# Paged keys of a decode step turned on VectorE in 32 by 32 blocks instead of on TensorE

## The chip, the cores and the metric

One core of one Trainium2 chip. The metric is the device time of one execution in microseconds, the median of several runs. All arithmetic is fp32, so each matmul stands in the trace as two MATMUL and two weight-load instructions (a transposition as one of each).

## The reference

Two layers of a hybrid decoder run over a prompt of 256 rows and over 8 sequences ("samples") that each add one token to 1024 cached ones. The cache is paged: 8 pages of 128 rows for each sequence. For the samples a layer computes two attentions over the cached keys, one attention over a band of the last 512 keys, and a compression of cached keys and values in blocks of 32 rows:

```python
full = jnp.concatenate([past_rows, rows], axis=1)
fdk, fdv, fik, fck, fcv, fsk, fsv = _split(full, CACHE_SPLITS)
yb = _dsa_attend(dq_h, iq_h, iw, qpos, fdk, fdv, fik)          # scores q . fdk
ck = _compress(fck, cmp_pe[0], cmp_w1[0], cmp_b1[0], cmp_w2[0])
cv = _compress(fcv, cmp_pe[1], cmp_w1[1], cmp_b1[1], cmp_w2[1])
o_cs = _nsa_cmp_sel(nq_h, qpos, ck, cv, fsk, fsv)              # scores q . fsk
o_w = _window_attend(nq_h, qpos, wk, wv, pos0 + L - lw)        # scores q . wk, 512 keys

def _compress(kv, pe, w1, b1, w2):
    blk = kv[:, idx] + pe[:, None, :]        # 63 blocks of 32 rows, step 16
    return jax.nn.silu(blk @ w1 + b1) @ w2
```

Keys have two heads of 64 columns, so a page has 128 columns of each of fdk, fsk, fck and fcv; there are 8 query heads for each sequence.

## The kernel before

Each engine has its own program, written out by hand, and they meet at semaphores (named steps such as "T 7", "C 7", "h 2"). A layer runs: the norm (ScalarE squares L1378, TensorE sum over partitions L782, ScalarE logarithm and exponential L1380 and L1382, VectorE scaling L1748), projections of slabs of w_in (L814), prompt work with gate projections (`mix`, L967) between its pieces, the page stage, the samples' softmax and output, the branches (L1322) and the output projection (L1340). Slabs of weights rotate through three slots; SP sends the slab for a slot once the last user of the slab three places before in the list STREAM is done.

**The page stage** is a loop over NW = 40 windows, 5 for each sequence. Four of them take a pair of pages each, the fifth takes the band of 512 keys.

- SP loads the even pages and POOL the odd ones into four slots `kst` (L549, L550: 64 KB and 192 KB each). A slot is loaded again as soon as TensorE has turned what it held ("T w").
- TensorE, in a page window: 8 transpositions of 128x128 (L1220), 4 of attention keys (into bank 3 or 5) and 4 of compression rows (into bank 4 or 6); then the scores of the window before, against its turned keys `KT` (L1175, L1179: 2 matmuls with 128 rows, 64 queries and 256 columns, one for each half of the output partitions). In a band window: 4 transpositions (L1224).
- ScalarE copies the turned keys from PSUM to `KT` (128x512, L1365), and half of the compression rows (two copies of 64x256, L1365) into `cT`; VectorE copies the other half (two of 64x256, L2125). TensorE may turn window w only when the copies of window w-2 are done.
- Compression goes by pairs of sequences: once a pair is in `cT`, TensorE multiplies it by `w1` in the page windows of the next sequence (`compress`, L1190: 4 matmuls of 256 columns in each of 4 windows). ScalarE moves one half of the result (`shift`), VectorE adds it (`join`, L2116), ScalarE applies SiLU (`hidden`, L1625), TensorE multiplies by `w2` (`compressed`, L1198, L1202), ScalarE takes the result. The last pair's `compress` has nothing beside it (L1190, 16 matmuls), and its end, "h 3", releases the loads of the values of sequences 4 to 7 (L556, L567), because they overlap `cT`.
- VectorE does some comparing for the sparse attention's choice of keys between its copies (L1931 to L1961).

ScalarE's first copy into `cT` of a layer waits until the second of two spills of gate projections (POOL, L741) has landed.

Of the kernel before, what the change touches and what calls it, by code (L numbers as in the profile page):

```python
# [14 lines left out]
ALU = mybir.AluOpType  # L15
# [3 lines left out]
D = 1024  # L19
LP = 256  # L20
NS = 8
# [7 lines left out]
NH = 8  # L29
# [13 lines left out]
NU = 5  # L43
NW = NS * NU
# [60 lines left out]
STREAM = ([n for n in FRONT + BACK + GATES if n in SLAB_OF] + [s[0] for s in GATE_SLABS] + [s[0] for s in OUT_SLABS])  # L105
NSLOT = 3


def slab_dmas(name):

    if name in SLAB_OF:
# [100 lines left out]
def hybrid_step(nc, x_prompt, x_sample, cache_kv, page_table, state_win, state_hgrn, norm_g, w_in,  # L212
# [4 lines left out]
    with ctx:  # L217
# [108 lines left out]
        cT = at(8192, 2, 2, ST, 4 * NBLK)  # L326
        Vw = at(16384, NS, 4, 128)
        kst = at(18432, 4, 2, 512)
        kws = at(22528, 2, 4, 128)
        KT = at(23552, 2, 512)  # L330
        hbd = at(24576, 8, NCS)[0:HD]
        hsd = at(25080, 8, NCS)[0:HD]
        hid = at(25584, 2, 2, 2, NCS)[0:HD]
# [21 lines left out]
        spill = nc.dram_tensor("spill", [2, 128, KD * LT], F32, kind="Internal").ap()  # L355
        xr = at(24000, 2, D)
# [17 lines left out]
        class Steps:  # L374
# [15 lines left out]
            def mark(self, step):  # L390
# [15 lines left out]
        first_in, lb_in = sem("first_in"), sem("lb_in")  # L406
        nx_p = Steps("nx_p", [f"xT {k}" for k in range(KD)])
# [42 lines left out]
        pg_p = Steps("pg_p", sum([[f"T {w}"] + [f"s {w - 1}"] * (w > 0) for w in range(NW)], []) + [f"s {NW - 1}"])  # L450
        pg_a = Steps("pg_a", sum([[f"K {w}"] + [f"C {w}"] * (w % NU < 4) for w in range(NW)], []))
        pg_v = Steps("pg_v", [f"C {w}" for w in range(NW) if w % NU < 4])
        GR = list(range(NS // 2))
        dc_p = Steps("dc_p", sum([[f"h {g}", f"w {g}"] for g in GR[:-1]], [])
                     + ["h 3", "new", "w 3", "s cmp", "t cmp", "imp", "group imp", "PT", "oT"])
        dc_v = Steps("dc_v", [f"sum {g}" for g in GR] + ["s cmp", "n cmp", "ptx cmp", "imp", "drop", "masked", "new p", "scaled", "ev"])
        dc_a = Steps("dc_a", sum([[f"hb {g}", f"hid {g}", f"c {g}"] for g in GR[:-1]], []) + ["scores", "hb 3", "hid 3", "c 3"]
# [53 lines left out]

        def blocks_of(s, k, u):

            return cT[halves[u], s // 2 % 2, :, :, :].rearrange("p v t (g b n) -> p v g b n t", g=2, b=2)[:, :, :, s % 2, 16 * k:16 * k + 16, :]
# [43 lines left out]
        def first_keys(engine, l, odd, pages):  # L558
# [3 lines left out]
            load_values(engine, l, 0, odd, pages)  # L562

# [6 lines left out]
        def _(sp):  # L570
# [21 lines left out]
            for l in range(DEPTH):  # L592
                l1 = bass.ds(l, 1)

                def send(name):
# [5 lines left out]
                    if at_ >= NSLOT:  # L601

                        old = STREAM[at_ - NSLOT]
                        if old in SLAB_OF:
                            sp.wait_ge(proj_ready, l * NJOB + LAST_JOB[old])
                        elif old[0] == "m":
# [50 lines left out]
                for name in ("m13", "m20", "m21", "m22"):  # L657
                    send(name)
                sp.wait_ge(cp_v.sem, cp_v(l, "prompt done"))
                for s in range(NS):  # L660
# [5 lines left out]
                    if s >= 2:  # L666
                        sp.wait_ge(pg_p.sem, pg_p(l, f"T {(s - 2) * NU + 4}"))
                    sp.dma_start(kws[:, s % 2, :, :], sw[:, :, 0:128]).then_inc(win_in[s % 2], 16)
                    if s in (2, 4, 6):
                        load_values(sp, l, s // 2, 0, pages)  # L670

                sp.wait_ge(dc_p.sem, dc_p(l, "h 3"))
                for s in range(4, NS):
                    load_values(sp, l, s, 0, pages)
                for name in ("m23", "b00", "b01"):
                    send(name)
# [19 lines left out]
        def _(pool):  # L696
# [8 lines left out]
            for l in range(DEPTH):  # L705
# [31 lines left out]
                for a in range(2):  # L737
                    pool.wait_ge(mx_a.sem, mx_a(l, f"m {8 * a + 7}"))
# [9 lines left out]
                for s in range(NS):  # L748
# [4 lines left out]
                    if s in (2, 4, 6):  # L753
# [1537 lines left out]
```

## Time and profile before

| | us |
|---|---|
| median of 3 runs | 1210.1 |
| lowest and highest | 1209.66, 1226.07 |
| the profiled execution, device time | 1212.78 |
| its span, first to last instruction | 1210.8 |
| TensorE matmul busy | 1115.8 (92%) |
| VectorE busy | 557.1 (46%) |
| ScalarE busy | 442.6 (37%) |
| chain that ended last, share on TensorE | 74% |

Busy time of TensorE counts a matmul from start to end, and matmuls overlap, so 92% doesn't say that the array is full. What an engine costs at a place is read from the chain of waits: the time from one group of instructions to the next. The two layers have the same program; the second one's page stage lies 594 us after the first one's.

### The profile page before, as it was taken

How to read it: one execution, taken by the hardware profiler on the slowest of the kernel's cores; microseconds unless marked ns; L12 is line 12 of the kernel's file. 1: busy time of each engine (PE TensorE's matmuls, PEld its weight loads, DVE VectorE, ACT ScalarE, POOL GpSimd, SP SyncE). 2: the span in 40 equal slices, each digit the busy share in tenths (PEclk: the TensorE clock that was granted, in tenths of full speed). 3: DMA queues.
4: the chain of work that ended last, by engine and by line, in shares of the span. 5: the costliest groups of instructions: out<-in, count | busy, mean ns of one | idle time of the engine just before them, and what ended most of it. 6: DMA issues, size and time to landing. Idle time of an engine off the chain costs nothing.

```text
span 1210.8 us, 19137 instructions
## 1 busy us (share of the span) xinstructions
PE 1115.8 (92%) x6856; PEld 884.6 (73%) x6856; DVE 557.1 (46%) x1306; ACT 442.6 (37%) x882; POOL 188.7 (16%) x327
## 2 busy tenths in 40 slices
PE   6999998998898899899789999899989979989998
PEld 4887777876675667788578877698657656668887
DVE  2103277878565542314111134887876563432241
ACT  2123442246433775320011353322654256652100
POOL 0200040011111451400020001200202044422000
PEclk8999998999998999999899999999999999999999
DMA  6563257545465784855345633683636287837552
GB/s 174 156 138 109 86 177 245 138 115 158 124 187 169 237 239 127 244 166 150 87 106 157 144 117 88 232 206 105 179 94 199 90 255 226 252 102 210 164 146 71
DMA packets 242716, 192.79 MB, mean 159 GB/s; under 512 B 117822, under 2 KB 224350, under 8 KB 241342
## 3 DMA queue, kind: packets, MB, share of 16 engines
q1 hardware_dynamic: 227358, 140.38, 42.4%
q0 software_dynamic: 15264, 51.19, 13.0%
q8 instruction: 55, 0.90, 0.3%
q14 instruction: 39, 0.32, 0.1%
HBM read 179.10 MB, written 20.80 MB: 165 GB/s over the span
## 4 chain that ended last, share of the span: by engine, by line
PE 74%; ACT 8%; DVE 7%; issue 3%; DMA 2%; DVEq 2%; SPq 2%; ACTq 1%
PE ps L814 21%; PE ps L967 11%; PE ps L1322 7%; PE ps L1190 5%; PE ps L1340 5%; ACT arena L1365 4%; PE ps L1220 4%; PE ps L990 2%; PE ps L1175 2%; PE ps L1101 1%; DMA spill<-arena 1%; PE ps L1293 1%; SPq L526 1%; PE ps L857 1%; DVE top L1807 1%
## 5 line engine op out<-in xcount | busy, mean ns | idle before, releaser
L1365 ACT ACTIVATE arena<-ps 64x256 f32<-64x256 f32 (+9 forms) x374 | 204.9, 564 | 285.3 <-PE ps L1332 73.7
L814 PE MATMUL ps<-hT,slab 128*128 128x264 f32 (+1 forms) x1280 | 300.5, 393 | 9.0 <-DVE hT L1748 6.4
L814 PEld LDWEIGHTS ps<-hT,slab 128*128 128x128 f32 (+1 forms) x1280 | 244.7, 193 | 54.4 <-issue 9.4
L967 PE MATMUL ps<-hT,slab 128*128 128x264 f32 x768 | 184.3, 397 | 3.3 <-DVEq L2100 3.3
L967 PEld LDWEIGHTS ps<-hT,slab 128*128 128x128 f32 x768 | 146.5, 194 | 36.0 <-issue 6.8
L2125 DVE COPY arena<-ps 64x256 f32<-64x256 f32 x128 | 76.1, 594 | 88.8 <-PE ps L1220 87.4
L539 POOL DMA_DIRECT2D arena<-in_cache_kv_dram x64 | 34.5, 539 | 397.2 <-PE ps L911 240.8
L1322 PE MATMUL ps<-Y,slab 128*128 128x264 f32 x384 | 85.8, 386 | 0.0
L1220 PE MATMUL ps<-cst,arena 128*128 128x128 f32 x512 | 70.7, 284 | 16.2 <-ACT arena L1365 9.3
L1220 PEld LDWEIGHTS ps<-cst,arena 128*128 128x128 f32 x512 | 58.4, 144 | 34.3 <-ACT arena L1365 21.1
L1322 PEld LDWEIGHTS ps<-Y,slab 128*128 128x128 f32 x384 | 73.0, 190 | 12.5
L1759 DVE SCALAR_TENSOR_TENSOR arena<-arena,gains 128x264 f32<-128x264 f32 x26 | 11.0, 488 | 117.2 <-ACT arena L1437 117.2
L1340 PE MATMUL ps<-arena,slab 128*128 128x264 f32 x256 | 62.2, 400 | 2.3 <-DVEq L2243 2.3
L1190 PE MATMUL ps<-arena,w 128*128 128x256 f32 x256 | 62.9, 393 | 0.0
L1513 ACT ACTIVATE arena<-ps 128x264 f32<-128x264 f32 x48 | 18.7, 389 | 113.1 <-PE ps L967 112.5
L1340 PEld LDWEIGHTS ps<-arena,slab 128*128 128x128 f32 x256 | 50.1, 198 | 11.8 <-DVEq L2243 3.1
L1190 PEld LDWEIGHTS ps<-arena,w 128*128 128x128 f32 x256 | 47.0, 192 | 15.9 <-issue 10.4
L556 POOL DMA_DIRECT2D arena<-in_cache_kv_dram x64 | 45.2, 711 | 43.0 <-PE ps L1190 41.0
L549 POOL DMA_DIRECT2D arena<-in_cache_kv_dram x64 | 34.4, 538 | 109.2 <-PE ps L1175 56.7
L1560 ACT ACTIVATE arena<-arena,st 128x128 f32<-128x128 f32 (+1 forms) x96 | 42.4, 444 | 13.7 <-DVEq L2023 12.9
L1175 PE MATMUL ps<-arena,QC 128*64 128x256 f32 x256 | 42.7, 413 | 2.3 <-ACT arena L1365 2.3
L1365 ACT ACTIVATE Y<-ps 128x264 f32<-128x264 f32 x24 | 9.4, 390 | 93.5 <-PE ps L814 93.5
(380 smaller groups left out, 1385.7 us busy)
## 6 DMA issues: line engine op xcount, KB each, us to landing
slab<-in_w_in_dram SPq DMA_DIRECT2D x48, 1024.0 KB, 5.5
slab<-in_w_in_dram SPq DMA_DIRECT2D x80, 256.0 KB, 3.9
arena<-in_cache_kv_dram SPq DMA_DIRECT2D x64, 192.0 KB, 3.8
arena<-in_cache_kv_dram POOLq DMA_DIRECT2D x64, 192.0 KB, 3.9
arena<-in_cache_kv_dram SPq DMA_DIRECT2D x64, 128.0 KB, 5.1
arena<-in_cache_kv_dram POOLq DMA_DIRECT2D x64, 128.0 KB, 5.7
slab<-in_w_branch_dram SPq DMA_DIRECT2D x16, 512.0 KB, 5.6
slab<-in_w_out_dram SPq DMA_DIRECT2D x8, 1024.0 KB, 4.8
```

What stands on the lines that cost most here:

```text
L539: engine.dma_start(ikst[:, u, i, h * HD:h * HD + HD], page_rows(l, pages[2 * pair + h, i])[:, 256:320])\
L556: engine.dma_start(V[:, s, 2 * k + odd, :, :], key_and_selected(pg, 128)).then_inc(v_in[odd], 16)
L814: last = mm(ps[0:job[3], n % 2, 0:LT], v[:, k, job[2]:job[2] + job[3]], hT[:, k, :], start=(k == 0), stop=(k == KD - 1))
L967: last = mm(ps[:, bank, 0:LT], v[:, k, (d % 2) * 128:(d % 2) * 128 + 128], hT[:, k, :], start=(k == 0), stop=(k == KD - 1))
L1175: last = mm(ps[h, j // 2, (j % 2) * 256:(j % 2) * 256 + 256], QC[:, a, s * ROWS:(s + 1) * ROWS], KT[:, w % 2, a * 256:(a + 1) * 256], star ...
L1190: last = mm(ps[:, 7, kv * 256:(kv + 1) * 256], w1[:, kv, t, :], cT[:, g % 2, kv, t, :], start=(t == 0), stop=(t == ST - 1))
L1220: last = nc.tensor.transpose(ps[:, bank, o:o + 128], kst[:, u % 4, i, c:c + 128], ident)
L1322: last = mm(ps[:, d % 4, 0:LT], v[:, j, dd * 128:dd * 128 + 128], Y[:, a, j, :], start=(j == 0), stop=(j == 3))
L1340: last = mm(ps[:, d % 4, 0:LT], v[:, k, (d % 2) * 128:(d % 2) * 128 + 128], mT[:, k, :], start=(k == 0), stop=(k == KD - 1))
L1365: return A(out, in_, ACT.Copy, scale=scale)
L1560: A(x[:, j, :], x[:, j, :], ACT.Exp, bias=st[:, c + j:c + j + 1], accum_out=sa[:, c + j:c + j + 1])
L2125: last = TC(blocks_of(s, j, u)[:, :, 0], pairs_of(4 + 2 * (w % 2), 0, u))
```

## The change

**Keys.** The attention keys of pages are no longer turned by TensorE. VectorE turns `kst` in blocks of 32 by 32, within each group of 32 partitions, into `kD` (two transpositions of 128x256 for a page window, step "D u"), and the band of a sequence in one transposition of 128x512 (step "W s"). After that, partition 32r+x holds column 32c+x of the tokens of row group r. Scores of a sequence are made at once, in `page_scores(s)`: for each of 4 column chunks c, each of 4 row groups r and each of 2 attentions a, one matmul with 32 rows, 32 queries and 256 (a=0) or 384 columns (a=1: pages and band), into bank r at the quarter 2a + s//4. It is called in the second window of the next sequence and waits for "W s". Its queries lie in `QR`, which POOL builds (a memset of 2048 columns, 16 copies) in a weight slot: the name "qr" is put into STREAM ahead of "m21", so later slabs move by one slot, "m22" is sent after the page stage, and "m23" waits for the last scores.

**Windows.** 32 windows, 4 for each sequence; 4 transpositions in each (compression rows only, banks 4 and 5). A `kst` slot is loaded again after both "T u" and "D u". ScalarE has no copy to `KT`.

**Compression** goes by sequence: 4 matmuls of 128 columns in every window of the next sequence, two banks (6 and 7) by turns, `compressed` for each sequence but the last two inside the loop. `cT` is halved.

**Values.** Those of sequence 1 are loaded during the prompt's work (`second_values`), of 2 and 3 at sequences 3 and 5.

**Elsewhere.** TensorE does 9 matmuls on a tile of zeros at the start and 7 at the start of each layer, before it waits for the first scaled hT (`keep_busy`). ScalarE does one dummy logarithm at the start of each layer.

```diff
+            pe.wait_ge(idle_set, 1)
+            keep_busy(5, 9)
...
+                                    if k == 0:
+                                        keep_busy(5, 7)
                                     pe.wait_ge(norm_v.sem, norm_v(l, f"hT {k}"))
...
+                def page_scores(s):
+
+                    pe.wait_ge(pg_v.sem, pg_v(l, f"W {s}"))
+                    for c in range(4):
+                        for r in range(4):
+                            for a in range(2):
+                                out = ps[quarter[2 * a + s // 4], r, 0:(NPG + 4 * a) * 32].rearrange("p (n j) -> p n j", j=32)
+                                last = mm(out, queries_of(r, c, a, s), block_keys(s, a)[quarter[r], :, 32 * c:32 * c + 32],
+                                          start=s % 4 == 0 and c == 0, stop=s % 4 == 3 and c == 3)
+                    last.then_inc(pg_p.sem, pg_p.mark(f"s {s}"))
...
+                for u in range(NU):
+                    s, j = u // 4, u % 4
+                    for e in range(2):
+                        pe.wait_ge(page_in[j][e], (l * NS + s + 1) * 32)
+                    if u >= 2:
+                        taken_from(u - 2)
+                    for a, c in enumerate((128, 256)):
+                        for i in range(2):
+                            o = a * 256 + i * 128
+                            last = nc.tensor.transpose(ps[:, 4 + u % 2, o:o + 128], kst[:, j, i, c:c + 128], ident)
+                    last.then_inc(pg_p.sem, pg_p.mark(f"T {u}"))
+                    if s:
+                        if j == 2 and s >= 2:
+                            compressed(s - 2)
+                        compress(s - 1, j)
+                        if j == 1:
+                            page_scores(s - 1)
+                for part in range(2):
+                    compress(NS - 1, part)
+                page_scores(NS - 1)
+                for part in range(2, 4):
+                    compress(NS - 1, part)
+                compressed(NS - 2)
...
                 if s:
-                    engine.wait_ge(pg_p.sem, pg_p(l, f"T {(s - 1) * NU + k}"))
+                    engine.wait_ge(pg_p.sem, pg_p(l, f"T {u - 4}"))
+                    engine.wait_ge(pg_v.sem, pg_v(l, f"D {u - 4}"))
...
+                A(spare[:, :], epsb[:, :], ACT.Ln)
...
+                ve.wait_ge(spill_out[0], l * 16 + 16)
+                for w in range(NU):
+                    s, j = w // 4, w % 4
+                    if s >= 2 and j == 0:
+                        ve.wait_ge(dc_p.sem, dc_p(l, f"h {s - 2}"))
+                    ve.wait_ge(pg_p.sem, pg_p(l, f"T {w}"))
+                    for u in range(2):
+                        last = TC(blocks_of(s, j, u)[:, :, 0], pairs_of(4 + w % 2, 0, u))
+                    last.then_inc(pg_v.sem, pg_v.mark(f"C {w}"))
+                    if s >= 2 and j == 0:
+                        ve.wait_ge(pg_p.sem, pg_p(l, f"s {s - 2}"))
+                    for a, c in enumerate((0, 384)):
+                        last = nc.vector.transpose(block_keys(s, a)[:, 2 * j:2 * j + 2, :], kst[:, j, :, c:c + 128])
+                    last.then_inc(pg_v.sem, pg_v.mark(f"D {w}"))
+                    if j == 3:
+                        ve.wait_ge(win_in[s % 2], (l * 4 + s // 2 + 1) * 16)
+                        nc.vector.transpose(block_keys(s, 1)[:, NPG:NPG + 4, :], kws[s % 2]).then_inc(pg_v.sem, pg_v.mark(f"W {s}"))
+                        if s:
+                            join(s - 1)
```

## Rows read from the trace of the kernel before

**Rows 1.** Page, first parts: busy us, share of the span, instructions

```profile
PE 1115.8 (92%) x6856; PEld 884.6 (73%) x6856; DVE 557.1 (46%) x1306; ACT 442.6 (37%) x882; POOL 188.7 (16%) x327
```

**Rows 2.** Stretches: us from start, length, busy (count) by engine, granted clock, DMA share, GB/s

```profile
379.00:485.00 106.00, 95.65 (x626) 67.56 (x628) 45.50 (x87) 72.00 (x125) 40.84 (x71) 0.98 0.70 211
```

**Rows 3.** The chain that ended last, page stage: start us, us, what

```profile
375.59 8.35 DMA spill<-arena
...
403.74 1.92 PE ps L1190 x8
405.67 0.87 PE ps L1220 x8
406.54 0.58 PE ps L1175 x4
...
428.84 1.93 PE ps L1190 x8
...
445.14 0.64 PE ps L1198 x4
445.78 0.60 PE ps L1202 x8
...
477.46 7.10 PE ps L1190 x32
```

**Rows 4.** Instruction groups of 379 to 485 us: busy us, mean ns | idle before

```profile
L1365 ACT ACTIVATE arena<-ps 64x256 f32<-64x256 f32 x66 | 39.7, 602 | 3.6 <-DMA spill<-arena 2.5
L2125 DVE COPY arena<-ps 64x256 f32<-64x256 f32 x64 | 38.0, 594 | 43.7 <-PE ps L1220 43.0
L1365 ACT ACTIVATE arena<-ps 128x512 f32<-128x512 f32 x40 | 23.8, 594 | 21.6 <-PE ps L1220 21.2
```

**Rows 5.** The chain elsewhere: full matmuls, four column groups

```profile
199.45 1.78 PE ps L990 x16
...
516.24 3.61 PE ps L1293 x128
```

**Rows 6.** Timeline of TensorE: a matmul in each of four row groups

```profile
370.38 0.73 PE L1158 MATMUL ps<-arena 24*128 24x264 f32 x8
```

**Rows 7.** Timeline of VectorE, instructions of 256 to 513 elements

```profile
390.84 0.41 DVE L1931 TENSOR_SCALAR tk<-tk,sgn,tkv 104x257 f32<-104x257 f32 x1
391.17 0.41 DVE L1932 TENSOR_SCALAR tk<-tk,sgn,tkv 104x257 f32<-104x257 f32 x1
...
398.77 0.69 DVE L1957 TENSOR_TENSOR_SCAN tk<-cst,tk 104x257 f32<-104x257 f32 x1
...
488.52 0.67 DVE L2157 TENSOR_REDUCE st<-arena 64x1 f32<-64x513 f32 x1
```

**Rows 8.** Page, DMA issues: KB each, us from issue to landing

```profile
arena<-in_cache_kv_dram POOLq DMA_DIRECT2D x64, 192.0 KB, 3.9
```

**Rows 9.** Timeline of POOL: a key load issued; a memset at the start

```profile
1.58 1.05 POOL L700 MEMSET QC<- 128x1152 f32 x1
...
404.45 0.55 POOL L549 DMA_DIRECT2D arena<-in_cache_kv_dram  x1
```

**Rows 10.** Start of each layer: first matmul (timeline), chain, one stretch

```profile
8.00 0.66 PE L790 MATMUL ps<-cst,arena 128*128 128x128 f32 x2 [8.00 <-DMA arena<-in_x_sample_dram]
...
15.51 6.18 PE ps L782 x16
...
24.64 21.08 PE ps L814 x80
...
25.00:30.00 5.00, 5.00 (x12) 3.77 (x12) 3.07 (x11) 0.21 (x1) 0.00 (x0) 0.50 0.10 15
...
619.25 1.28 ACT L1380
...
623.47 19.73 PE ps L814 x80
644.98 24.92 PE ps L814 x112
```

More of the change, by code:

```diff
@@ L42 @@
 ROWS = NS * NH
-NU = 5
-NW = NS * NU
+NU = NS * 4
 ST = CS // 2
@@ L355, in hybrid_step @@
         spill = nc.dram_tensor("spill", [2, 128, KD * LT], F32, kind="Internal").ap()
+        idle = at(30400, LT)
         xr = at(24000, 2, D)
@@ L656, in _ @@
                 first_keys(sp, l, 0, pages)
-                for name in ("m13", "m20", "m21", "m22"):
+                for name in ("m13", "m20"):
                     send(name)
+                second_values(sp, l, 0, pages)
+                send("m21")
                 sp.wait_ge(cp_v.sem, cp_v(l, "prompt done"))
@@ L770, in _, with keep_busy @@
             mm = nc.tensor.matmul
+            def keep_busy(bank, n):
+                for _ in range(n):
+                    mm(ps[:, bank, 0:LT], idle[:, 0:128], idle, start=True, stop=True)
+            pe.wait_ge(idle_set, 1)
+            keep_busy(5, 9)
             pe.wait_ge(first_in, 16)
@@ L1236, in _ @@
-                page_scores(NW - 1)
-                taken_from(NW - 2)
-                pe.wait_ge(dc_a.sem, dc_a(l, "c 2"))
-                for part in range(4):
-                    compress(3, part)
+                        mm(ps[:, b, 256:256 + NCS], w2[:, x, :], hid[:, 0, x, :], start=(x == 0), stop=(x == 1))
+                    for x in range(2):
+                        last = mm(ps[0:NCS, b, 320 + HD * x:384 + HD * x], hid[:, 1, x, :], w2[:, 2, 0:HD], start=True, stop=True)
+                    last.then_inc(dc_p.sem, dc_p.mark(f"w {s}"))
@@ new lines, in hidden, with take_compressed @@
+                def hidden(s):
+                    act.wait_ge(dc_v.sem, dc_v(l, f"sum {s}"))
+                    for kv in range(2):
+                        last = A(hid[:, kv], hsd[:, 2 * kv:2 * kv + 2, :], ACT.Silu, bias=hbias[0:HD, kv:kv + 1])
+                    last.then_inc(dc_a.sem, dc_a.mark(f"hid {s}"))
+                def take_compressed(s):
+                    act.wait_ge(dc_p.sem, dc_p(l, f"w {s}"))
+                    copy(ckd[:, s, :], ps[:, 6 + s % 2, 256:256 + NCS])
+                    copy(CV[0:NCS, s, :], ps[0:NCS, 6 + s % 2, 320:448]).then_inc(dc_a.sem, dc_a.mark(f"c {s}"))
@@ L1658, in _ @@
+                hidden(NS - 2)
+                act.wait_ge(pg_p.sem, pg_p(l, f"s {NS - 1}"))
+                for a, x in ((0, SS[:, 0:PAST]), (1, SW[0:ROWS, 0:WIN])):
+                    n = (NPG, 4)[a]
+                    rows = slice(HD, 128) if a else slice(0, 128)
+                    copy(x.rearrange("p (n r j) -> p r n j", n=n, r=4),
+                         ps[rows, 0:4, a * 256:a * 256 + n * 32].rearrange("p r (n j) -> p r n j", n=n), SCALE)
                 act.drain().then_inc(dc_a.sem, dc_a.mark("scores"))
-                shift(3)
+                shift(NS - 1)
@@ L1704, in rest @@
                 ve.memset(spare[:, :], 0.0)
+            ve.memset(idle, 0.0)
+            ve.drain().then_inc(idle_set, 1)
             ve.memset(epsb[:, :], EPS)
```

234 lines of the change are left out of this document (96 added, 138 removed).

## The prediction

> **What bounds the kernel now.** The page comes first. TensorE is busy in 92% of the span and VectorE in 46% [rows 1], so TensorE's path sets the time; the reader should ask what each stage's chain waits for. Next, the stretch of the page stage, 379 to 485 us: TensorE 95.65 of 106 us, ScalarE 72.00, VectorE 45.50, DMA share 0.70 [rows 2]. Then the chain of waits inside it [rows 3]: in windows with compression TensorE is the chain, 0.87 us for 8 transpositions, 0.58 for 2 score matmuls, 1.92 for 4 compression matmuls, 3.38 in all. In the windows between, ScalarE's copies stand in the chain. A pair of sequences takes from 403.74 to 428.84, and the next two pairs 24.5 and 24.1, so a sequence takes 12.25 us. The groups say why ScalarE is there: a window costs it two copies of 602 ns and one of 594 [rows 4], 1.8 us; VectorE waits 43.0 us for transpositions and has room. After the loop, 7.10 us of compression stand alone.
>
> **Part by part, TensorE in one sequence of the new loop.**
> - Transpositions: 16 in place of 36. 0.87 us for 8 is 0.11 each [rows 3], so 1.76 us.
> - Compression: 16 matmuls of 128 columns, 32 instructions. Full matmuls of 128 columns take 1.78 us for 16 instructions [rows 5], so 3.56 us; before it was 3.85 for a sequence. Nothing is gained here: the columns are the same.
> - Scores: 32 matmuls in tiles of 32 by 32, 8 tiles. The trace has no such form. Four column groups run side by side: 128 instructions of 128 columns in 3.61 us, 28 ns each, where a full one takes 111 [rows 5]. Four row groups too: 8 instructions of 264 columns in 0.73 us, where one after another at 222 ns each (24.92 / 112, [rows 10]) they would take 1.78 [rows 6]. If rows and columns combine, the longest tile sets the time: 4 chunks x 2 x 384 columns x 0.83 ns (from 222 / 264; 0.84) = 2.6 us. If only the row groups run side by side, both attentions add: 4 x 2 x 640 x 0.84 = 4.3 us. With 0.5 us for filling and for the change of tile shape I take 3.1, because both single forms reach the full factor of four. The bounds are 2.6 and 4.8.
> - `compressed`: 0.64 + 0.60 us for two sequences [rows 3]. Half the columns with the same latency: 0.8.
> - A first weight load that isn't hidden costs about 0.2 us at a change of shape (1.92 us for 8 instructions of 256 columns is 0.2 above 8 x 0.215). Two more of these: 0.4.
>
> The sum is 1.76 + 3.56 + 3.1 + 0.8 + 0.4 = 9.6 us; I take 9.7 where before it was 12.25.
>
> **The others in one sequence.** ScalarE: 8 copies of 0.60 and about 1.6 of small ones, 6.4 us, no longer near. VectorE: 8 copies of 0.594, 4.8 us. The transposition is in no row. From below: instructions of 257 elements follow each other after 0.33 us, and one of 513 takes 0.67 [rows 7]. From above: the copy of 256 elements out of PSUM at 0.60 [rows 4] and the scan at 0.69 [rows 7]. SBUF to SBUF on one source is nearest to the first, so 0.35 for 256 and 0.65 for 512: 8 x 0.35 + 0.65 = 3.45, and `join` 0.4, as an instruction of its 252 elements [rows 7]. VectorE needs 8.65 us, 1.0 less than TensorE. Inside the sequence it fits: from the end of the last transposition to "W s" there are 1.2 + 0.7 + 0.65 = 2.55 us, and TensorE has 3.55 us of transpositions and compression before the scores ask for it.
>
> The Trainium skill ("VectorE: DVE Perf Modes", The three transpose paths) gives 311 ns for 128x128 in bf16 on VectorE; no run here shows it, and twice the elements at one per cycle more would be an estimate of 0.45 us, which would put VectorE at 9.6 us, level with TensorE.
>
> The Trainium skill ("TensorEngine Tiling (Array Packing)", Key Properties) says that a change of tiling mode drains the array; the 0.2 us steps in the trace agree in sign. The same notes ("TensorE: Matmul & The Clock Gate", Part 3) give 6.32 times for 9 tiles; an estimate at 5.6 times for 8 tiles would be 64 instructions of on average 267 ns / 5.6 = 3.1 us.
>
> **The start of the stage.** ScalarE's first copies wait for the spill in both kernels, until 383.96 (375.59 + 8.35) [rows 3]. From 385.7, the third transposition, VectorE has no pause until compression of sequence 1 can begin: 5 windows of 1.9, 1.2 for the copies of the sixth, one band 0.65, and the comparing, 5.5 us (45.50 less 38.0 of copies and some 2 of joins [rows 2, 4]). That is 16.9 us, so 402.6; before, compression began at 403.74. Little changes here, and the work that hid VectorE's comparing is gone.
>
> **The sum for a layer.** The windows of sequence 2 begin at about 402.3; 6 x 9.7 us lead to 460.5. The tail: half of the compression after the last copies, scores, the other half, 1.2 + 1.8 + 3.1 + 1.8 less the 0.9 that overlaps = 7.0, so 467.5, where before it ends at 484.56 (477.46 + 7.10). One more `compressed` 0.8 stands before the softmax part, the last one is 0.5 shorter: 16.7 us saved. From that I take 1.7 for loads that come late when the values of sequences 2 and 3 join the keys (the stage's mean is 211 GB/s at a share of 0.70 [rows 2]; the same bytes in 17 us less make it 0.83, and these bursts lie above the mean). 15 us for a layer, 30 for both.
>
> At no cost: QR on POOL (1.9 us of memset, by 1.05 for 1152 columns [rows 9], and 16 copies, about 4 us) lies in the prompt's last 16 us before the stage; without that cover its 6 us would delay the scores. "m22" is sent behind 16 value loads of SP and used by the fourth `mix` after the loop, behind the samples' first softmax; uncovered it would cost some us there. Values of sequence 1 load in the prompt's part.
>
> **The start of the layers.** The sum over partitions takes 6.18 us for 16 instructions; at 222 ns they would take 3.6. The first 80 projections take 21.08 and 19.73 us, where 80 x 222 ns = 17.8 [rows 10]: the granted clock is 0.50 of full, 1.2 GHz, in 25 to 30 us, after TensorE had waited 3 us for the norm. 2.6 + 3.3 + 1.9 us can be won, and 0.5 from the logarithm's table load at 619.25. The 9 matmuls must be over when x arrives at 8.0 us [rows 10]; 18 x 0.44 us at 1.2 GHz would end at 9.4. The 7 take 14 x 0.222 = 3.1 us, as long as the wait. I take 6 of the 8.3 us.
>
> 30 + 6 = 36 us off 1212.78, the profiled execution's own device time; that stands 2.7 above the median. So 1210.1 - 35 = 1175 us.
>
> **The rivals.**
> - *Scores only in row groups.* Against it speaks that column groups with different moving data run at four times [rows 5]. Price: 1.7 us x 7 sequences x 2 = 24: 1198 us (1 in 8).
> - *Pages come late.* A slot is now released by VectorE. After a window's transposition come copies and turning 1.9 us, with the next window's or the band in front of it up to 3 more; then POOL issues two loads of 0.55 and 3.9 us pass until they land [rows 8, 9]: 0.44 + 1.9 + 1.9 to 3.0 + 5.0 = 9.3 to 10.3 us for the second slot, about the period itself. For it: nothing is left over. Against: the other slots have 2 us more. Price: 0.6 us x 8 x 2 and the bursts: 1187 us (1 in 7).
> - *VectorE becomes the bound.* If turning costs what a copy from PSUM costs, 0.60 for 256 and 1.2 for 512, a sequence takes 4.8 + 4.8 + 1.2 + 0.4 = 11.2 us. Price: 1.5 x 7 and 3 at the start, x 2 = 27: 1202 us (1 in 8).
> - *Slower: VectorE turns fp32 far below one element per cycle.* At 1.0 us for 256 elements a layer's 80 units of 256 cost 0.65 x 80 less 7 of slack = 45 us more than forecast: 1265 us. It decides from 0.81 us on, 0.12 above the slowest row of that length [rows 7]. 1 in 20.
> - *The zeros buy nothing*, since the transpositions after them are sparse: 1181 us, inside the likeliest case.
>
> **How the numbers follow.** The likeliest case, 1160 to 1186 us, has 0.52. Its low end is 2.6 for the scores, no late load and the whole gain at the start. Late pages 0.15, half of it below 1186; row groups only 0.12; VectorE's bound 0.12; slower 0.05; 0.04 for a wait not seen. The range 1160 to 1200 takes in the first three and the low part of the fourth. The bound for faster, 2% or about what a measurement of this kernel can tell, is 1185.9: faster 0.61, within 0.33, slower 0.06.
>
> **What would show it.** In the changed kernel's chain a sequence should take 9.7 us in the loop with TensorE as most of it; 64 score instructions 3.1 us; a transposition of 128x256 0.35 to 0.41 us, of 128x512 about 0.65; VectorE idle about 1 us in each sequence; no wait of TensorE for a cache load; "h 7" about 16 us earlier in the stage than "h 3"; the 80 first projections near 18 us. Wrong would be: score groups of 4 us or more, a VectorE without idle time, or TensorE waiting for pages.

## The result

The median was 1220.4 us over 20 runs, where the kernel before took 1212.3 us in runs beside it: a ratio of 1.0063, 95% interval 1.0039 to 1.0088. The forecast was 1175 us. The change is half a per cent slower, by more than the interval, and not 3% faster.

### The profile page after: what moved, and what is told of

Its sections match the earlier page's. It is cut to its first block, busy times and chain, and to the rows that moved or that the text cites. A ratio compares the mean times of both kernels' runs of the same rounds, so it can differ in the third digit from the quotient of the medians.

```text
span 1219.0 us, 20778 instructions
## 1 busy us (share of the span) xinstructions
PE 1104.7 (91%) x7574; PEld 896.9 (74%) x7574; DVE 623.4 (51%) x1459; ACT 408.0 (33%) x841; POOL 201.1 (17%) x361
## 3 DMA queue, kind: packets, MB, share of 16 engines
q0 software_dynamic: 15264, 51.19, 12.8%
## 4 chain that ended last, share of the span: by engine, by line
PE 70%; DVE 7%; DMA 7%; SPq 5%; ACT 4%; issue 3%; DVEq 3%; ACTq 1%
PE ps L859 21%; PE ps L1012 10%; PE ps L1356 7%; PE ps L1374 5%; PE ps L1236 4%; DMA slab<-in_w_in_dram 3%; PE ps L1220 3%; PE ps L1035 2%; DMA arena<-in_cache_kv_dram 2%; SPq L572 2%; PE ps L1260 2%; ACT arena L1399 2%; PE ps L1146 1%; DMA spill<-arena 1%; PE ps L1327 1%
## 5 line engine op out<-in xcount | busy, mean ns | idle before, releaser
L859 PE MATMUL ps<-hT,slab 128*128 128x264 f32 (+1 forms) x1280 | 296.6, 389 | 2.7 <-DMA slab<-in_w_in_dram 2.7
L859 PEld LDWEIGHTS ps<-hT,slab 128*128 128x128 f32 (+1 forms) x1280 | 242.1, 191 | 46.2 <-DMA slab<-in_w_in_dram 3.1
L1399 ACT ACTIVATE arena<-ps 64x256 f32<-64x256 f32 (+15 forms) x316 | 167.5, 552 | 309.9 <-PE ps L1260 78.2
L1012 PE MATMUL ps<-hT,slab 128*128 128x264 f32 x768 | 191.2, 408 | 9.5 <-DMA slab<-in_w_in_dram 7.3
L1012 PEld LDWEIGHTS ps<-hT,slab 128*128 128x128 f32 x768 | 150.7, 200 | 45.5 <-DMA slab<-in_w_in_dram 8.1
L2162 DVE COPY arena<-ps 64x256 f32<-64x256 f32 x128 | 82.5, 644 | 41.1 <-PE ps L1260 39.7
L1236 PE MATMUL ps<-arena,w 128*128 128x128 f32 x512 | 79.3, 306 | 16.3 <-DVE arena L2162 9.7
L1236 PEld LDWEIGHTS ps<-arena,w 128*128 128x128 f32 x512 | 71.7, 217 | 21.2 <-DVE arena L2162 19.2
L1260 PE MATMUL ps<-cst,arena 128*128 128x128 f32 x256 | 46.2, 312 | 25.0 <-issue 11.0
L1374 PE MATMUL ps<-arena,slab 128*128 128x264 f32 x256 | 62.1, 400 | 2.3 <-DVEq L2288 2.3
L1260 PEld LDWEIGHTS ps<-cst,arena 128*128 128x128 f32 x256 | 33.6, 159 | 37.1 <-issue 32.1
L1374 PEld LDWEIGHTS ps<-arena,slab 128*128 128x128 f32 x256 | 50.0, 198 | 11.7 <-DVEq L2288 3.1
L2167 DVE STREAM_TRANSPOSE arena<-arena 128x256 f32<-128x256 f32 x128 | 49.3, 424 | 2.0
L1596 ACT ACTIVATE arena<-arena,st 128x128 f32<-128x128 f32 (+1 forms) x96 | 42.4, 445 | 13.6 <-DVEq L2060 12.8
L1220 PE MATMUL ps<-arena,slab 32*32 32x384 f32 (+1 forms) x1024 | 46.6, 446 | 0.0
```

The source lines that it names most:

```text
L859: last = mm(ps[0:job[3], n % 2, 0:LT], v[:, k, job[2]:job[2] + job[3]], hT[:, k, :], start=(k == 0), stop=(k == KD - 1))
L1012: last = mm(ps[:, bank, 0:LT], v[:, k, (d % 2) * 128:(d % 2) * 128 + 128], hT[:, k, :], start=(k == 0), stop=(k == KD - 1))
L1220: last = mm(out, queries_of(r, c, a, s), block_keys(s, a)[quarter[r], :, 32 * c:32 * c + 32], start=s % 4 == 0 and c == 0, stop=s % 4 == 3 ...
L1236: last = mm(ps[:, 6 + s % 2, kv * 128:(kv + 1) * 128], w1[:, kv, t, :], cT[:, s % 2, kv, t, :], start=(t == 0), stop=(t == ST - 1))
L1260: last = nc.tensor.transpose(ps[:, 4 + u % 2, o:o + 128], kst[:, j, i, c:c + 128], ident)
L1374: last = mm(ps[:, d % 4, 0:LT], v[:, k, (d % 2) * 128:(d % 2) * 128 + 128], mT[:, k, :], start=(k == 0), stop=(k == KD - 1))
```

## The profile after

The lines of the changed kernel are numbered anew: L859 is projection, L1012 `mix`, L1260 the transpositions of a page window, L1220 the scores, L1236 `compress`, L1245 and L1247 `compressed`, L1327 the samples' output, L1374 the output projection, L810 the matmuls on zeros, L2162 VectorE's copies.

First the page, busy time by engine (against [rows 1]): TensorE lost 11 us of busy time, and the span (1219.0 us) is 8.2 us longer. So TensorE waits more.

```profile
PE 1104.7 (91%) x7574; PEld 896.9 (74%) x7574; DVE 623.4 (51%) x1459; ACT 408.0 (33%) x841; POOL 201.1 (17%) x361
```

Then the chain that ended last (start us, us, what), to be laid beside [rows 3, 5, 10]:

```profile
20.26 17.82 PE ps L859 x80
...
370.05 8.27 DMA spill<-arena
...
402.31 3.34 PE ps L1220 x46
416.09 5.20 DMA arena<-in_cache_kv_dram
421.29 2.04 issue
...
427.82 2.74 PE ps L1220 x46
441.10 6.55 DMA arena<-in_cache_kv_dram
...
477.39 2.00 PE ps L1236 x16
488.73 15.37 DMA slab<-in_w_in_dram
504.14 3.83 PE ps L1012 x16
...
515.68 5.28 PE ps L1327 x128
...
615.59 3.57 PE ps L1374 x16
621.20 4.59 DMA slab<-in_w_in_dram
625.83 4.84 PE ps L810 x14
630.67 17.80 PE ps L859 x80
```

The reader subtracts the two chains at places that both have. After less before:

| place | before | after | difference |
|---|---|---|---|
| spill, ahead of the page stage | 375.59 | 370.05 | -5.5 |
| last compression of the stage ends | 484.56 | 479.39 | -5.2 |
| 128 matmuls of the samples' output | 516.24 | 515.68 | -0.6 |
| last output projection of layer 1 | 614.75 | 615.59 | +0.8 |
| first projection of layer 2 | 623.47 | 630.67 | +7.2 |

The start of layer 1 gained what it should. The page stage, where 15 us were forecast, gained nothing in layer 1: 109.0 us from the start of the spill to the end of the last compression before, 109.3 after. Then 6 us are lost behind the stage, and 6.4 us between the layers. Layer 2 is a little better inside the stage (107.6 us, before 110.8) and loses 5.2 us behind it; at its end the span is 8.2 us longer.

**Inside the stage.** The timeline of TensorE (start us, us, group, idle before it) shows the first of two such places:

```profile
418.44 0.60 PE L1260 MATMUL ps<-cst,arena 128*128 128x128 f32 x4
418.88 1.06 PE L1236 MATMUL ps<-arena,w 128*128 128x128 f32 x8
423.33 0.63 PE L1260 MATMUL ps<-cst,arena 128*128 128x128 f32 x4 [3.39 <-issue]
423.79 1.71 PE L1236 MATMUL ps<-arena,w 128*128 128x128 f32 x8
425.29 1.06 PE L1260 MATMUL ps<-cst,arena 128*128 128x128 f32 x4
```

TensorE waits 3.39 us for a page of keys. The chain leads to a key load of 5.20 us that was issued behind the values of sequence 2 (four loads on each queue; issuing them alone takes SP 2.55 us and POOL 2.83), and it gives the last 2.04 us to "issue", for which it names no releaser. That the values are the cause is shown by e_vals and e_spread, below. After the wait the same 8 compression instructions take 1.71 us instead of 1.06 and 4 transpositions 1.06 instead of 0.60. The stretches show the clock (length, busy by engine, granted clock, DMA share, GB/s):

```profile
413.20:423.40 10.20, 6.81 (x98) 5.21 (x98) 7.70 (x16) 4.46 (x9) 7.58 (x13) 1.00 1.06 317
424.00:428.00 4.00, 4.00 (x30) 3.81 (x35) 3.51 (x7) 3.32 (x6) 1.07 (x2) 0.57 0.82 248
448.00:452.00 4.00, 3.17 (x15) 3.20 (x16) 1.94 (x4) 1.89 (x4) 0.00 (x0) 0.50 1.05 327
515.60:521.00 5.40, 5.40 (x138) 4.74 (x141) 0.00 (x0) 0.00 (x0) 0.00 (x0) 0.68 0.45 169
```

In the burst the DMA share is 1.06 at 317 GB/s. After the wait the granted clock is 0.57, and after the second such wait, of 4.01 us, it is 0.50 (1.2 GHz). These two waits are paid twice: once themselves, once in what follows at the lower clock.

**Behind the stage.** "m22" is requested at 488.73, behind 16 loads of values, and takes 15.37 us, where the slab at 621.20 takes 4.59. TensorE waits 3.40 us for it, until 504.14, and the 128 matmuls of the output at 515.68 take 5.28 us instead of 3.61 [rows 5], at a granted clock of 0.68. Between the two lie 11 us at 1.00, so here the lower clock doesn't follow the wait at once. In layer 2 it does: after a wait of 3.9 us the next 16 instructions of `mix` take 5.51 us instead of 3.76, at a clock of 0.70, and the 128 take 3.61.

**Between the layers.** TensorE is done with layer 1 at 619.16. A slab of layer 2 is requested at 621.20 and lands at 625.8. The seven matmuls on zeros stand behind the wait for that slab, so they run after it, in 4.84 us at a clock of 0.69 (3.12 us in layer 1). Before, the projections began 5.2 us after the last output projection [rows 10]; now 11.5.

## Experiments

Three edits each remove one suspected wait from the changed kernel, a fourth adds the start alone to the kernel before. Each ratio is to the kernel before, executed beside it, with a 95% interval.

### e_rot: the slots turn on

The change put "qr" into STREAM. SP reused slots by the place in the list modulo three, anew in each layer. With 46 names (46 = 3 x 15 + 1) the first slab of layer 2 falls into the slot of the last one of layer 1.

```diff
-    _s = _i % NSLOT
+        _s = (_i + _l * len(STREAM)) % NSLOT
```

> The changed kernel with one thing altered: the three weight slots rotate on across the layers (slot = position in the list of both layers, modulo 3), so the first slab of the second layer takes the slot of o1, not of o3. Theory (the extra name qr makes the list 46 long, so that slab waits for the last output projection, and the 7 matmuls on zeros then stand behind it): the second layer's first projection comes 6 to 7 us earlier, 1213 to 1214 us where the changed kernel has 1220.4. Rival (the second layer's start waits for the norm chain anyway): 2 us or less.

Measured: 1213.9 us, ratio to before 0.9999 (0.9968 to 1.0030), 7.7 us less by the ratios and as expected. The chain of e_rot:

```profile
618.00 3.57 PE ps L1387 x16
623.25 3.12 PE ps L822 x14
626.36 17.83 PE ps L872 x80
```

The projections begin 4.8 us after the last output projection. The wait for the slab is gone, and the zeros take 3.12 us, within the wait for the norm.

### e_m22: the slab ahead of the values

```diff
+                send("m22")
                 sp.wait_ge(dc_p.sem, dc_p(l, "h 7"))
                 for s in range(4, NS):
                     load_values(sp, l, s, 0, pages)
-                for name in ("m22", "m23", "b00", "b01"):
+                for name in ("m23", "b00", "b01"):
```

> The changed kernel with one thing altered: SP sends the slab m22 before the values of sequences 4 to 7, as soon as its slot is free, not behind them. Theory (TensorE's 3.4 us wait for m22 in each layer and what the array's clock loses by it are the late slab): 6 to 8 us less than the changed kernel, 1213 us. Rival (the loads after the page stage are bound by bytes, so the wait only moves to the values): no change, 1219 to 1221 us, with TensorE waiting for cache loads ahead of L1327.

Measured: 1211.05 us, 0.9998 (0.9970 to 1.0027), 7.9 us less by the ratios; the theory holds. Its chain has no transfer behind the stage, and the 128 matmuls are back at 3.61 us:

```profile
506.03 3.76 PE ps L1013 x16
...
512.13 3.61 PE ps L1328 x128
```

### e_vals: values 2 and 3 before the stage

Both queues load the values of sequences 2 and 3 before the stage instead of at sequences 3 and 5.

```diff
-                    if s in (3, 5):
-                        load_values(sp, l, s // 2 + 1, 0, pages)
...
+                for s in (2, 3):
+                    load_values(sp, l, s, 0, pages)
                 send("m21")
```

> The changed kernel with one thing altered: the values of sequences 2 and 3 are loaded before the page stage (SP behind those of sequence 1, POOL behind the second spill), not inside it. Theory (the two waits of 3.4 and 4.0 us for pages, and the half clock for some 4 us after each, come from the value loads that stand in front of the key loads): both waits go, 16 to 22 us less in all, 1199 to 1204 us. Rival (keys come late because a slot is released by VectorE's turning): waits of the same length stay, 1216 to 1220 us.

Measured: 1206.6 us, 0.9953 (0.9921 to 0.9986), 13.3 us less by the ratios, where 16 to 22 were expected. Its chain:

```profile
378.96 9.59 DMA arena<-in_cache_kv_dram
...
416.30 2.74 PE ps L1225 x46
426.60 2.74 PE ps L1225 x46
436.94 2.74 PE ps L1225 x46
```

The waits in mid-stage are gone and the clock stays at 1.00 from 416 to 447 us. A new one of 5.2 us stands at the stage's start: the keys of sequence 1 now come behind 16 pages of values. And the undisturbed sequence takes 10.3 us, not 9.7. That is a second error, of another kind (below).

### e_start: the start alone, in the kernel before

The zeros and the dummy logarithm of the change, put into the kernel before:

```diff
+            pe.wait_ge(idle_set, 1)
+            keep_busy(5, 9)
...
+                                    if k == 0:
+                                        keep_busy(5, 7)
```

> The kernel before with only the parts at the layers' start: 9 matmuls on zeros at the beginning, 7 ahead of the first projection of each layer, and the dummy logarithm. Theory: the start gains what the changed kernel shows there, 7.6 us in the first layer and 2 in the second, where no slab is late: 1202 to 1204 us against 1212.3 of the kernel before. Rival (work behind it is paced by loads and takes the gain back): 1208 us or more.

Measured: 1207.0 us, 0.9952 (0.9917 to 0.9987), 5.8 us less. That is between the theory's 1202 to 1204 and the rival's 1208, so neither held. Its chain is 8.0 us ahead of the kernel before at 38 us, 3.1 ahead of the page stage, and not at all inside it (compression begins at 403.89 against 403.74); at 600 us it is 2.3, layer 2's start brings it to 4.5, the span to 5.4. Layer 2's page stage keeps its lead of 6.0. What took the lead of layer 1 back isn't shown.

### e_all: all three, and e_nokeep: without the zeros

> The changed kernel with the three edits of e_rot, e_m22 and e_vals together: the slab slots go on turning from layer 1 to layer 2, m22 is sent ahead of the values of sequences 4 to 7, and the values of sequences 2 and 3 are loaded before the page stage. Theory (the three waits stand at three places, so what each took away adds up): 7 us from the start of layer 2, 8 to 9 us from m22, 13 us from the values, from 1220 down to about 1192 to 1196, ratio to the kernel before 0.984 to 0.988; the copy of m22 is no longer waited for, and the first projection of layer 2 follows 4 us behind the last instruction of layer 1. Rival (the transfers share one bandwidth, so a wait taken from one place comes back at another): the saving is no more than that of the best single edit, 1205 to 1208, and waits for DMA show at the start of the page stage or at its end.

Measured: 1191.8 us, 0.9824 (0.9751 to 0.9898). The single edits took 0.0064, 0.0065 and 0.0110 off the changed kernel's 1.0063, together 0.0239; e_all took 0.0239. That they agree to the last digit is luck, since the interval of e_all is 0.0074 to each side, 9 us. But the rival's 1205 to 1208 is out (the slowest of four executions took 1193.7): the three waits are separate, and most of what each took away stays away.

e_nokeep is e_all without its `keep_busy` calls.

```diff
-            keep_busy(5, 9)
...
-                                        keep_busy(5, 7)
```

> As e_all, without the instructions that keep TensorE running on zeros ahead of the first transposes and of each layer's first projection (their results are used by nothing). It tells what these are worth in a kernel in which the waits are gone. Theory (the gain at a layer's start is kept, except for what the clock gives back later, as e_start against the kernel before showed: 7.9 us at 38 us into the span, 5.4 at its end): 4 to 7 us slower than e_all; the first 80 instructions of projection take 19 to 21 us instead of 17.8 in both layers, at a granted clock below 1.0. Rival (with the waits gone TensorE has no more stretches at the lower clock later that could give back anything, or the start of layer 2 is warm without them): 8 to 11 us, or under 3 us.

Measured: 1202.0 us, 0.9899 (0.9823 to 0.9976), so 10.2 us slower by the medians and 12.8 by the spans; my 4 to 7 us was too little, the rival's 8 to 11 fits the medians. The dummy logarithm is still in it. The chains, first e_nokeep, then e_all:

```profile
23.98 18.04 PE ps L877 x80
...
618.25 19.73 PE ps L877 x80
```

```profile
19.86 17.82 PE ps L878 x80
...
609.57 17.83 PE ps L878 x80
```

In layer 1 it is 4.1 us behind at the first projection and 4.3 after it, at layer 2 8.7 and then 10.6. The 19 to 21 us expected for the 80 projections came in layer 2 alone; in layer 1 they took 18.04. What of the rest is the zeros and what the spread of single executions stays open: at 350 us, where their code is still the same, e_noturn and e_take (both below) lie 6.3 us apart.

### e_spread: one page of values at a time

From e_all; the values of sequences 2 and 3 go one page behind every third page of keys, from sequence 2 to 7.

```diff
+            n, rest = divmod(w - 8 - odd, 3)
+            if rest or not 0 <= n < 8:
+                return
+            b, k = 2 + n // 4, n % 4
+            pg = page_rows(l, pages[b, 2 * k + odd])
+            engine.dma_start(V[:, b, 2 * k + odd, :, :], key_and_selected(pg, 128)).then_inc(v_in[odd], 16)
```

> As e_all, but the values of sequences 2 and 3 are neither loaded at once before the stage nor in two bursts inside it: one page of values goes behind every third page of keys on each of the two queues, from sequence 2 to sequence 7. Theory (what cost time in the stage was the burst, eight value pages of 128 KB ahead of the next key pages, and not the bytes; and what e_vals paid at the stage's start, up to 5 us of waiting per layer for the keys of sequence 1, was again a burst): the period stays at 10.3 to 10.4 us per sequence, no key page is waited for in mid-stage, the wait at the stage's start goes, and it is 4 to 8 us faster than e_all. Rival (the bytes count: e_vals moved 229 to 234 GB/s at a DMA share of 0.77 to 0.81 in that stage, and this adds about 35 GB/s): key pages come late by small amounts, the period becomes 10.6 to 11 us, and it is no faster than e_all.

Measured: 1185.4 us, 0.9769 (0.9696 to 0.9842), 6.4 us below e_all by the medians and 3.8 by the spans. The period (the time from one sequence's scores to the next's) is 10.33 us, and no key page is waited for in the first layer's stage; in the second, one sequence takes 10.76. The changed kernel loads the same bytes in the same stage and waits 3.39 and 4.01 us: it was the burst that cost, not the bytes.

The wait at the stage's start is gone too, but it pays less. e_all waits there 4.9 us for keys and then 2.64 for VectorE's copies; e_spread waits twice for VectorE's copies instead:

```profile
385.65 2.08 PE L1257 MATMUL ps<-arena,w 128*128 128x128 f32 x8 [2.22 <-DVE arena L2183]
399.28 1.16 PE L1257 MATMUL ps<-arena,w 128*128 128x128 f32 x8 [2.63 <-DVE arena L2183]
```

From the last `mix` before the stage to its end e_spread is some 2 us shorter in each layer.

### e_order: which partitions are written at once

From e_all. In the changed kernel ScalarE's and VectorE's pairs of copies start together in two of four windows and take 1.40 to 1.47 us there; apart from each other they take 1.16 to 1.25. Both write partitions 0 to 63 first, then 64 to 127.

```diff
-                    for u in range(2):
+                    for u in (1, 0):
                         last = copy(blocks_of(s, j, u)[:, :, 1], pairs_of(4 + w % 2, 1, u))
```

> As e_all, but ScalarE takes its two copies of a key page in the other order, so that the two engines, which start together, write different halves of the partitions (VectorE partitions 0 to 63 while ScalarE writes 64 to 127, then the reverse). It tells why a pair of copies takes 1.43 to 1.47 us where both engines start together and 1.20 us where they don't. Theory (they disturb each other where they write the same partitions of SBUF): the pairs take 1.20 to 1.25 us also where they start together, the wait of compression for the last copy falls from 0.74 us to about 0.5, the period from 10.3 to about 10.05 us, 3 to 4 us over both layers. Rival (they disturb each other by reading the same PSUM bank, or because TensorE writes while they read): the pairs stay at 1.4 to 1.5 us, the period at 10.3, the time that of e_all.

Measured: 1182.5 us, 0.9738 (0.9666 to 0.9811). The timelines, first e_all (VectorE apart, then VectorE and ScalarE together, then the wait of TensorE), then e_order with the same:

```profile
422.51 1.19 DVE L2181 COPY arena<-ps 64x256 f32<-64x256 f32 x2
...
427.28 1.41 DVE L2181 COPY arena<-ps 64x256 f32<-64x256 f32 x2 [0.88 <-PE ps L1279]
...
427.27 1.45 ACT L1418 ACTIVATE arena<-ps 64x256 f32<-64x256 f32 x2 [2.56 <-PE ps L1279]
...
431.76 1.13 PE L1255 MATMUL ps<-arena,w 128*128 128x128 f32 x8 [0.71 <-ACT arena L1418]
```

```profile
430.51 1.19 DVE L2181 COPY arena<-ps 64x256 f32<-64x256 f32 x2 [0.88 <-PE ps L1279]
...
430.51 1.21 ACT L1418 ACTIVATE arena<-ps 64x256 f32<-64x256 f32 x2 [2.57 <-PE ps L1279]
...
434.77 1.13 PE L1255 MATMUL ps<-arena,w 128*128 128x128 f32 x8 [0.49 <-ACT arena L1418]
```

Pairs that start together take 1.2 us now, and the period falls from 10.31 to 10.08 us, as the theory had it. The PSUM partitions that each engine reads are the same as before. The edit also changes which of two neighbouring PSUM columns ScalarE reads at that time; that it is the writing alone isn't separated from this. The medians of e_order and e_all differ by 9 us, the spans by 2.4, and the periods account for 3 to 4; the rest of the 9 is not explained.

### e_best and e_noturn

e_best joins e_spread and e_order.

> The changed kernel with slots that turn on, m22 ahead of the values, the values of sequences 2 and 3 spread page by page (e_spread), and ScalarE's copies in the other order (e_order). Theory (the spread took 6.4 us off e_all, the order 9.3 us by the medians but only 3 to 4 us by the periods in its profile, 10.08 instead of 10.31 us over some 13 sequences): 3 to 4 us below e_spread, 1181 to 1183 us, ratio to the kernel before 0.973 to 0.976, period 10.05 to 10.1 us. Rival (what the median of e_order showed adds up in full): 1175 to 1177 us. Third (with a shorter period and value pages in the stream the pages of keys come late): period 10.3 us or more and no gain on e_spread.

Measured: 1182.7 us, 0.9754 (0.9727 to 0.9781), the first theory: 2.7 us below e_spread. From spill to the end of the stage it takes 96.9 and 97.3 us in the two layers, e_spread 98.6 and 98.5. It isn't below e_order, though (0.9738, 0.9666 to 0.9811). So by the medians the spread and the order don't add up; by the traces they do, at 3 to 4 us each. Differences of a few us between kernels of four to six executions aren't decided by their medians.

e_noturn leaves most of the turning out from sequence 2 on, so most keys of those sequences' pages are left out of the computation:

```diff
-                        last = nc.vector.transpose(block_keys(s, a)[:, 2 * j:2 * j + 2, :], kst[:, j, :, c:c + 128])
+                            last = nc.vector.transpose(block_keys(s, a)[0:32, 2 * j:2 * j + 1, 0:32], kst[0:32, j, 0:1, c:c + 32])
```

> As e_best, but from sequence 2 on VectorE turns only one 32 by 32 block where it turned a whole page pair: the keys of pages that are scored there are left out of the computation by it, the keys of the window are still turned. It tells whether the turning, 0.77 us for each of the 32 page pairs of a layer, costs time where it lies. Theory (it lies behind VectorE's copies, while TensorE waits for ScalarE's copies of the last pair of a sequence, 0.49 us in e_order, and page slots are free long enough ahead): the period stays at 10.0 to 10.1 us and the time within 3 us of e_best, although VectorE's busy time falls by some 2.5 us a sequence. Rival (VectorE's turning holds up the copies or the page slots): the period falls to 9.6 us, the sum of TensorE's own work, 5 to 6 us in all.

Measured: 1184.6 us, 0.9779 (0.9753 to 0.9806). Its chain and, from the groups of 400 to 480 us, the small transpositions that are left:

```profile
422.57 2.74 PE ps L1241 x46
432.65 2.74 PE ps L1241 x46
```

```profile
L2191 DVE STREAM_TRANSPOSE arena<-arena 32x32 f32<-32x32 f32 x48 | 7.0, 178 | 0.8
```

The period is 10.08 us with or without. VectorE's turning costs no time in the loop at this period. The run says nothing on a shorter period, nor on the stage's start: there sequences 0 and 1 are still turned, and there TensorE waits for VectorE.

### e_take: two small copies earlier

The wait that is left, 0.49 us in each sequence, is put down to ScalarE. Its program takes the compressed rows of sequence s-2 behind the two copies of the last window; they free the PSUM bank for the next sequence's compression.

```diff
+                    if s >= 2 and j == 3:
+                        take_compressed(s - 2)
                     act.wait_ge(pg_p.sem, pg_p(l, f"T {w}"))
...
-                    if s >= 2 and j == 3:
-                        take_compressed(s - 2)
```

> As e_best, but ScalarE takes the compressed rows of sequence s-2 (two small copies) before it waits for the last transposition of sequence s, not behind the two copies of 64x256 that follow that transposition. In e_best the first compression matmul of each sequence waits 0.49 us for ScalarE (0.74 in e_all); it may start only when the compressed rows are out of its PSUM bank. Theory (the small copies, which could have run a microsecond earlier, are what ends that wait): the wait goes, the period falls from 10.08 to 9.6 us, which is TensorE's own work, and over 6 sequences of both layers the time falls by 5 to 6 us, to 1176 to 1178. Rival (the copies of the page themselves end that wait, and the small ones finish with them): the period stays at 10.0 to 10.1 us, the time at 1182 to 1184. Third (at 9.6 us pages of keys come late): single waits for a cache load of a microsecond or more, a gain of under 3 us.

Measured: 1183.7 us, 0.9754 (0.9701 to 0.9807). The chain and the stretches:

```profile
416.85 2.74 PE ps L1241 x46
426.49 2.74 PE ps L1241 x46
436.88 2.74 PE ps L1241 x46
446.52 2.74 PE ps L1241 x46
```

```profile
420.00:430.00 10.00, 9.96 (x124) 8.08 (x123) 8.69 (x19) 6.35 (x14) 5.45 (x10) 1.00 0.88 261
430.00:440.00 10.00, 9.35 (x120) 7.60 (x119) 8.58 (x18) 5.90 (x13) 5.81 (x11) 1.00 1.01 298
```

The wait is gone, and an undisturbed sequence takes 9.64 us (416.85 to 426.49, 436.88 to 446.52). So the first theory was right on the cause and wrong on the time: between them lies a sequence of 10.39, in which TensorE stands idle for 0.66 us ahead of a page's transpositions, in a stretch of DMA share 1.01 at 298 GB/s (the timeline puts this down to issue, as it does the 3.39 us above). In layer 2 the sequences take 9.64, 11.22, 9.63 and 10.40 us. From spill to the end the stage takes 94.9 and 96.9 us, 2.0 and 0.4 less than in e_best, which no median shows. The third answer, late pages, took the gain.

Why that page is late is partly in the timelines of e_take, VectorE, POOL and TensorE:

```profile
426.75 0.77 DVE L2188 STREAM_TRANSPOSE arena<-arena 128x256 f32<-128x256 f32 x2
428.23 0.54 POOL L586 DMA_DIRECT2D arena<-in_cache_kv_dram  x1 [1.54 <-DVE arena L2188]
433.84 0.63 PE L1281 MATMUL ps<-cst,arena 128*128 128x128 f32 x4 [0.66 <-issue]
```

TensorE was done with the slot at 424.0, VectorE turned it only at 426.75 to 427.52, and POOL, which had waited 1.54 us for that, issued the load at 428.23. So VectorE, not TensorE, set when the slot came free, 3.5 us later. From the issue of the load's second part (428.83) to TensorE's start lie 5.0 us, where the median from issue to landing for 192 KB from POOL is 4.2 us between 405 and 460 us, so slower transfers may have a share too. No run separates the two.

## Why the forecast was wrong, point by point

**The costs of the new instructions were right.** 64 score instructions take 2.74 us in the chain at full clock (3.0 to 3.3 us where the clock is lower, as at 402.31), against 3.1 (2.6 to 4.8): row and column groups do combine, and the rival of row groups only falls. VectorE turns 128x256 in 0.42 us and two in 0.77, and 128x512 in 0.67, against 0.35 and 0.65. The two rivals on VectorE's price fall too, and e_noturn shows that the turning costs nothing in the loop at 10.08 us.

**TensorE's own sum was right, partly by luck, and the period was wrong.** The sum of 9.6 us for a sequence is what e_take runs at when undisturbed, 9.64. But its terms cancel: the scores took 0.4 us less than forecast, and the transpositions (1.91 us) and `compressed` (0.95) 0.15 more each. The forecast period left out a wait of 0.70 to 0.74 us. The step that failed is "ScalarE, 6.4 us, no longer near". ScalarE was busy for 6.6 us of a sequence, so the share was right, but it was read where an order had to be read. Two small copies of ScalarE stood in its program behind the last window's copies, and those take 1.45 us, not 1.20, when both engines start together.

**The start of the stage and its tail were short by 3 to 4 us for a layer.** From the spill's landing to the compression of sequence 1 the forecast had 18.4 us (402.3 less 383.94); e_spread took 21.1, with the two waits for VectorE above. VectorE's copies, turning and comparing there were put at 16.9 us; they lasted from 380.64 to 399.23, 18.6. The tail took 8.0 us, not 7.0. No experiment took VectorE's work away there.

**Late loads of values were put at 1.7 us for a layer.** This is the largest error: by the ratios 13.3 us came off with e_vals, and 4 (spans) to 6 (medians) more with e_spread, so 8.5 to 10 us for a layer. The argument by a mean share of 0.83 was the wrong one; the share measured over the stage is 0.66. The page stage has few slots, and a burst of 8 pages of values ahead of the next keys in the same queues made these land 3.4 and 4.0 us late. Nor did the forecast count what follows such a wait, the clock of 0.50 to 0.57.

**"m22" at no cost, "uncovered it would cost some us".** The cover was named (the samples' first softmax) and not measured. 16 value loads lie ahead; request to landing took 15.4 us. e_m22: 7.9 us by the ratios, both layers.

**The start of layer 2 was not followed past the added name.** The prediction said that slabs move by one slot, and did not count 46 modulo 3 at the layer's border. e_rot: 7.7 us, once. The zeros, 3.1 us "as long as the wait", then stand behind that slab and take 4.84 at the lower clock.

**The start of layer 1 was right.** 21.08 us became 17.82, and the sum over partitions 3.61; the first projections end 7.6 us earlier. e_start gives 5.8 us for both layers in the kernel before, against 6 forecast, e_nokeep 10 in the changed one.

**The rival "pages come late"** named the wrong cause for what was measured: with e_vals no page is late in the loop at 10.3 us, so there a slot that VectorE releases is released in time. At the 9.7 us of the forecast it would have been partly right. It put the time from one use of a slot to the next at 9.3 to 10.3 us; in e_take the slot turned at 423.4 is turned again at 433.8, 10.4 us later, after the late release by VectorE.

Of the 45 us between forecast and result (1175 and 1220) the three waits make 29, and the burst that e_vals only moved 4 to 6. The rest, about 10, is the stage itself: from spill to end the forecast had 91.9 us before its late loads (467.5 less 375.59), and e_spread, in which the waits for loads are gone from layer 1, takes 98.6. Of these 6.6 us for a layer about 3 are the longer period, and 3 to 4 the start and the tail; the 1.7 that the forecast held back covers a part. The best kernel here, e_best, is at 0.9754 of the kernel before, 30 us, and so faster than both.

## What to carry to other kernels

Follow every name added to a rotating list to the border where the rotation begins again, and every transfer that is moved behind a burst by the burst's own length, not by the mean share. When an engine gets room, read its program for small work that others wait for, behind large work that nobody waits for yet. A mechanism can be worth its price and the kernel still be slower: here TensorE's own work came out as forecast, and most of what was lost was lost in the loads around it.

## What the runs showed of the hardware

- Eight tiles of 32 by 32, two column groups on each of four row groups, fp32: 64 instructions of 256 or 384 columns in 2.74 us, which is what 4 chunks x 2 x 384 columns alone take at 0.83 ns (2.6 us). The 256-column matmuls beside them cost no more than the 0.1 us between.
- Two engines that copy out of one PSUM bank, in different partitions, into the same SBUF partitions: 0.70 to 0.74 us a copy when together, about 0.60 when apart; with the order of one turned, 0.60 together. The Trainium skill ("SBUF — State Buffer", SBUF: two separate sides) says that within the engine side only the port pair that VectorE and GpSimd share causes contention. The runs differ from this for VectorE and ScalarE, as far as e_order separates it.
- After waits of TensorE for pages, of 3.4 and 4.0 us, the granted clock was 0.57 and 0.50 in the stretches of 4 us around the work that followed, which took 1.71 us instead of 1.06 for 8 instructions. These waits cost clearly more than their own length. After the 3.4 us wait for "m22" it was 1.00 for 11 us and then 0.68.
- Loads have a price before they move a byte: four value loads took SP 2.55 us and POOL 2.83 us to issue, and the key loads behind them in the same programs were issued only then.
